# Attention of three branches in pairs of heads, and half of the modulation on VectorE

## The reference, cut to what matters

```python
mod = silu(c) @ w_mod[l] + b_mod[l]            # 6 x 1024: sh1, sc1, ga1, sh2, sc2, ga2; the same with c_ctx
h = rms_norm(x, norm1_g[l]) * (1 + sc1) + sh1
(..., gq, gk, gv, wq, wk, wv, nq, nk, nv, gate) = split_projection(h @ w_in)
out_a = mlstm(...)                             # branch A
out_b = softmax(q @ k.T * d**-0.5) @ v         # B: 8 heads of 64, 2 key heads, rms norm and rotary on q and k
out_c = ...                                    # C: the same in a window, with a sink logit in the softmax
out_d = ...                                    # D: 8 heads with their own keys, neighbourhood bias
y = sum_b sigmoid(gate_b) * (out_b @ w_branch[b]);  x = x + ga1 * (y @ w_out)
h2 = rms_norm(x, norm2_g[l]) * (1 + sc2) + sh2
x = x + ga2 * moe_ffn(h2)                      # 32 experts, top 2
```

## Time and profile before

| | us |
|---|---|
| median of 3 runs | 3130.76 (3129.21 to 3133.28) |
| profiled execution | 3133.22 |
| its span | 3131.6 |
| TensorE busy (share of span) | 2776.3 (89%) |
| VectorE busy | 894.6 (29%) |
| ScalarE busy | 420.0 (13%) |
| granted TensorE clock, mean | 0.94 |
| DMA | 623.62 MB, 199 GB/s |

### The profile page before, as it was taken

How to read it: one execution, slowest core, us unless ns; L and a number is a source line. 1 busy time by engine, 2 the same in 40 slices (tenths; PEclk the granted TensorE clock), 3 DMA queues, 4 the chain that set the end, 5 groups by cost and what they waited for, 6 DMA issues and landing times.

```text
span 3131.6 us, 43741 instructions
## 1 busy us (share of the span) xinstructions
PE 2776.3 (89%) x18152; PEld 1686.2 (54%) x18153; DVE 894.6 (29%) x2317; ACT 420.0 (13%) x960; POOL 148.9 (5%) x246
## 2 busy tenths in 40 slices
PE   4999899999999959999999889999999858777882
...
GB/s 270 54 54 54 68 32 59 41 54 54 74 47 236 96 134 376 381 380 376 379 384 382 269 93 54 81 94 51 108 115 163 219 203 396 393 402 394 403 400 142
DMA packets 148709, 623.62 MB, mean 199 GB/s; under 512 B 9329, under 2 KB 13697, under 8 KB 131713
## 3 DMA queue, kind: packets, MB, share of 16 engines
...
HBM read 596.94 MB, written 25.28 MB: 199 GB/s over the span
## 4 chain that ended last, share of the span: by engine, by line
PE 74%; DMA 16%; DVE 6%; issue 3%; ACT 1%; POOL 1%; SPq 0%; DVEq 0%; ACTq 0%; POOLq 0%
DMA ring<-in_e_up_dram 12%; PE bank L1378 11%; PE bank L1167 11%; PE bank L1077 10%; PE bank L1386 7%; PE bank L1067 6%; PE bank L1178 5%; PE bank L1095 5%; PE bank L1224 4%; PE bank L1254 4%; PE bank L1371 3%; PE bank L1236 2%; PE bank L1297 2%; DMA ring<-in_e_down_dram 1%; PE bank L1361 1%
## 5 line engine op out<-in xcount | busy, mean ns | idle before, releaser
L1378 PEld LDWEIGHTS bank<-scr,ring 128*64 128x64 f32 x8192 | 341.8, 138 | 25.9 <-issue 25.8
L1378 PE MATMUL bank<-scr,ring 128*64 128x96 f32 x8192 | 348.0, 247 | 1.2 <-DVE scr L2021 1.2
L1371 PE MATMUL bank<-ring,scr 128*64 128x256 f32 x2048 | 266.0, 419 | 89.4 <-DMA ring<-in_e_up_dram 70.3
L1167 PE MATMUL bank<-HT,ring 128*128 128x512 f32 (+1 forms) x1024 | 342.7, 490 | 0.0
L1077 PE MATMUL bank<-ring,HT 128*128 128x512 f32 (+1 forms) x800 | 303.6, 536 | 1.2 <-ACT ring L795 1.2
L1371 PEld LDWEIGHTS bank<-ring,scr 128*64 128x64 f32 x2048 | 156.8, 150 | 203.2 <-DMA ring<-in_e_up_dram 77.1
L1167 PEld LDWEIGHTS bank<-HT,ring 128*128 128x128 f32 x1024 | 191.3, 191 | 122.5 <-issue 110.1
L1386 PE MATMUL bank<-ring,scr 128*96 128x512 f32 x512 | 225.1, 592 | 0.8 <-issue 0.8
L1077 PEld LDWEIGHTS bank<-ring,HT 128*128 128x128 f32 x800 | 152.2, 194 | 134.3 <-issue 128.3
L1095 PE MATMUL bank<-ring,scr 128*128 128x512 f32 x384 | 175.8, 615 | 50.4 <-DMA ring<-in_w_mod_dram 34.8
L1067 PE MATMUL bank<-HT,ring 128*128 128x512 f32 (+1 forms) x512 | 199.1, 549 | 5.1 <-ACT scr L795 3.6
...
## 6 DMA issues: line engine op xcount, KB each, us to landing
ring<-in_e_up_dram SPq DMA_DIRECT2D x64, 2048.0 KB, 11.5
ring<-in_e_down_dram SPq DMA_DIRECT2D x64, 2048.0 KB, 11.6
ring<-in_e_gate_dram SPq DMA_DIRECT2D x64, 2048.0 KB, 9.2
ring<-in_w_in_dram SPq DMA_DIRECT2D x34, 2048.0 KB, 7.8
ring<-in_w_mod_dram SPq DMA_DIRECT2D x24, 2048.0 KB, 8.1
ring<-in_w_branch_dram SPq DMA_DIRECT2D x8, 2048.0 KB, 7.7
...
ring<-in_w_out_dram SPq DMA_DIRECT2D x4, 2048.0 KB, 7.9
```

Of the source, the lines that this page charges most:

```text
L1167: m = pe.matmul(bank[:, 0:NQ], w[:, k, (ft % 4) * P:(ft % 4) * P + P], HT[:, k, 0:NQ], start=k == 0, stop=k == KT_D - 1)
L1371: m = pe.matmul(ps[bank][hf * HALF:hf * HALF + cap, 0:256], XTv[:, k, :], w[:, k, hf * 256:hf * 256 + 256], start=k == 0, stop=k == KT_D - 1)
L1378: m = pe.matmul(ps[bank][rows_, f * cap:f * cap + cap], w[:, k, f * P + hf * HALF:f * P + hf * HALF + HALF], XTv[:, k, :], start=k == 0, s ...
```

## The change

- Stages D, B and C take heads in pairs. In D a pair is heads 2j and 2j+1, in B and C heads j and j+4, so that the two lie in the lower and the upper 64 partitions of the operands. A stage has 16 pair items in layer 0 and 8 in layer 1, and one step more than items.
- Scores: one matmul per head, each in its half of the array's rows, into two banks of one tile (`score_banks`). There is one pair of score banks, one buffer of P (`PB`) and one of turned P (`PTP`).
- P is scaled by the reciprocal before it is turned (`normalise`). ScalarE alone copies the turned blocks, both heads at once. The values are the stationary operand, 64 columns, each head in its half of the array's columns; the result is already transposed and VectorE copies it into `OT`. The `ot` transposes of D, B and C and their copies are gone. `OT` of D and C lies where `O` of stage A lay.
- Step i on TensorE: `turn(i-1)`, `scores(i)`, half of the due groups, `values(i-1)`, the other half.
- The eight `mod_b` groups are gone from stage C. VectorE multiplies rows of `w_mod` by `csil` and adds them up in `ACC`, 16 instructions of 512 columns per block in layer 0 (two vectors, 8 row groups each) and 8 in layer 1 (one vector, in two parts), four blocks in stage B and four in C. TensorE sums `ACC` over partitions with a matrix of ones. VectorE adds a row of `b_mod`, GpSimd stores the row to memory, and after all eight loads them back, spread over partitions.
- The third slot of the ring holds the two halves (1 MB each) of these blocks in stages B and C; the other weight blocks have two slots there. SP's order is sorted by the step in which a slot comes free. The value weights of B and C come in two transfers of 64 partitions. `out` 0 and 1 go to fixed slots.

```diff
-HOLD = {"A": 2, "D": 0, "B": 0, "C": 0}
-HEADS = {"A": MH, "B": 8, "C": 8, "D": 8}
+HOLD = {"A": 2}
+PAIRS = 4
...
+def sum_blocks(l, b):
+
+    if b not in "BC":
+        return []
+    todo = [(l, n) for n in range(4, 12)]
+    half = len(todo) // 2
+    return todo[:half] if b == "B" else todo[half:]
...
+def sum_span(l, b, j):
+
+    steps, n = stage_steps(l, b) - 1, len(sum_blocks(l, b))
+    return j * steps // n, (j + 1) * steps // n
...
+def sum_list(l, b, j):
+
+    m, n = sum_blocks(l, b)[j]
+    return [(k, part) for k in range(KT_D if m < L - 1 else KT_D // 2) for part in range(2)]
...
-        return value + gate + [("mod_b", n) for n in range(8)]
+        return value + gate
...
+def n_items(l, b):
+
+    return (MH if b == "A" else PAIRS) * q_tiles(l)
...
+    return n_items(l, b) + (2 + HOLD[b] if b == "A" else 1)
...
+        OT_B = br(6144, 2048).rearrange("p (j n) -> p j n", j=4)
+        OT = {"A": OT_A, "D": OT_B, "B": OT_A, "C": OT_B}
...
+        ACC = br(WK + 2048, 1024).rearrange("p (s n) -> p s n", s=2)
+        ROW = br(WK + 3072, 512)
...
+        SP_ = ctx.enter_context(nc.psum_tensor("score_banks", [P, 2, 512], F32))
+        PT_ = ctx.enter_context(nc.psum_tensor("turned_banks", [P, 2, 512], F32))
...
+                if slot is None:
+                    slot = sum(1 for k in BLOCK if k[0] == l) % (2 if key[1] in LATE else N_SLOT)
...
+            LATE = ("wq", "wk", "valD", "gateB", "valB", "gateC", "valC", "out")
...
+                slot = (1 - BLOCK[l, "valC"][0], N_SLOT - 1)[n]
...
+                def load_row(b, j):
+
+                    m, n = sum_blocks(l, b)[j]
+                    pool.dma_start(ROW, ins["b_mod"][m, n * 512:n * 512 + 512].partition_broadcast(P)).then_inc(row_loaded, 16)
+
+                def store_row(b, j):
+
+                    m, n = sum_blocks(l, b)[j]
+                    at = sum_index(l, b, j)
+                    pool.wait_ge(row_ready, at + 1)
+                    for s_ in range(2):
+                        pool.dma_start(mod_dram[m][s_:s_ + 1, n * 512:n * 512 + 512],
+                                       ROW[s_ * HALF:s_ * HALF + 1, :]).then_inc(row_stored, 16)
+                    pool.wait_ge(row_stored, 32 * (at + 1))
+
+                pool.wait_ge(o_ready, 4 * l + 2)
+                for b in "BC":
+                    for j in range(len(sum_blocks(l, b))):
+                        load_row(b, j)
+                        store_row(b, j)
+                for s_ in range(2 if l < L - 1 else 1):
+                    rows_ = slice(s_ * HALF, s_ * HALF + HALF)
+                    pool.dma_start(MODB[rows_, :], mod_dram[l][s_, 2 * D:5 * D].partition_broadcast(HALF)).then_inc(mod_loaded, 16)
+                    pool.dma_start(GA2[rows_, :], mod_dram[l][s_, 5 * D:6 * D].partition_broadcast(HALF)).then_inc(mod_loaded, 16)
...
+                    def turned_copy(i):
+
+                        c = c0 + i
+                        w = 512 if todo[i][1] < 2 else 256
+                        act.wait_ge(pair_turned, c + 1)
+                        if c:
+                            act.wait_ge(pair_out, c)
+                        act.activation(PTP[:, :, 0:w], PT_[:, :, 0:w], ACT.Copy).then_inc(pair_pt, 1)
+
+                    def exponentials(i):
+
+                        c = c0 + i
+                        lo = 0 if todo[i][1] < 2 else 256
+                        at = 2 * (c % 2)
+                        act.wait_ge(pair_peak, c + 1)
+                        if b == "C":
+                            act.activation(esink[:, at:at + 2], esink[:, at:at + 2], ACT.Exp)
+                        for hf in range(2):
+                            last = act.activation(PB[:, hf, 0:512 - lo], SP_[:, hf, lo:512], ACT.Exp, bias=nms[:, at + hf:at + hf + 1],
+                                                  scale=0.125, accum_out=rsum[:, at + hf:at + hf + 1])
+                        last.then_inc(pair_exp, 1)
...
+                def modulation_sum(b, j):
+                    pe.wait_ge(acc_ready, sum_index(l, b, j) + 1)
+                    both = l < L - 1
+                    def mms(bank):
+                        for s in range(2):
+                            at = s * HALF if both else 0
+                            m = pe.matmul(bank[at:at + HALF, :], ones[:, 0:HALF], ACC[:, s, :],
+                                          start=both or s == 0, stop=both or s == 1)
+                        return m
...
+                        lo = 0 if q < 2 else 256
+                        if c:
+                            pe.wait_ge(pair_exp, c)
+                        for hf in range(2):
+                            s = hf * HD
+                            k_ = KT_[s:s + HD, j, lo:512] if b == "D" else KT1[s:s + HD, lo:512]
+                            m = pe.matmul(SP_[:, hf, lo:512], QT_[s:s + HD, j, q * P:q * P + P], k_, start=True, stop=True)
+                        m.then_inc(pair_scored, 1)
+
+                    def turn(i):
+                        c = c0 + i
+                        pe.wait_ge(pair_p, c + 1)
+                        if c:
+                            pe.wait_ge(pair_pt, c)
+                        for hf in range(2):
+                            for k in range(4 if todo[i][1] < 2 else 2):
+                                m = pe.transpose(PT_[:, hf, k * P:k * P + P], PB[:, hf, k * P:k * P + P], ident)
+                        m.then_inc(pair_turned, 1)
+
+                    def values(i):
+                        j, q = todo[i]
+                        c = c0 + i
+                        pe.wait_ge(pair_pt, c + 1)
+                        if c >= 2:
+                            pe.wait_ge(pair_done, c - 1)
+                        tiles = range(4) if q < 2 else (2, 3)
+                        for n_, s in enumerate(tiles):
+                            for hf in range(2):
+                                at = j * P + hf * HD if b == "D" else P + hf * HD
+                                v = (V_ if b == "D" else KV)[:, s, at:at + HD]
+                                m = pe.matmul(ps[2 + c % 2][hf * HALF:hf * HALF + HALF, 0:P], v, PTP[:, hf, n_ * P:n_ * P + P],
+                                              start=n_ == 0, stop=n_ == len(tiles) - 1)
+                        m.then_inc(pair_out, 1)
+
+                    for i in range(n + 1):
+                        if i:
+                            turn(i - 1)
+                        if i < n:
+                            scores(i)
+                        if i == n and b in "DB":
+                            operands_transposed("B" if b == "D" else "C")
+                        for j in sums_at(l, b, i):
+                            modulation_sum(b, j)
+                        groups = due(l, b, i)
+                        half = (len(groups) + 1) // 2
+                        fill(b, groups[:half])
+                        if i:
+                            values(i - 1)
+                        fill(b, groups[half:])
...
+                def accumulate(b, j, ops):
+
+                    at = sum_index(l, b, j)
+                    both = l < L - 1
+                    for k, part in ops:
+                        if k == 0 and part == 0 and at:
+                            g = G[prev_sum(at)]
+                            dve.wait_ge(dense_full, g + 1)
+                        if sum_ops[0] >= 2:
+                            dve.wait_ge(acc_step, sum_ops[0] - 1)
+                        acc = ACC[:, part, :]
+                        c = csil[:, part if both else 0, (k if both else 2 * k + part):(k if both else 2 * k + part) + 1]
+                        row = k if both else 2 * k + part
+                        hf = row // 4
+                        dve.wait_ge(half_full[hf], HALF_BLOCK[l, b, j, hf])
+                        x = half_view(hf)[:, row % 4, :]
+                        if k == 0:
+                            m = dve.tensor_scalar(acc, x, c, None, ALU.mult)
+                        else:
+                            m = dve.scalar_tensor_tensor(out=acc, in0=x, scalar=c, in1=acc, op0=ALU.mult, op1=ALU.add)
+                        m.then_inc(acc_step, 1)
...
+                def sum_rows(b, i):
+
+                    for j in sums_at(l, b, i):
+                        at = sum_index(l, b, j)
+                        both = l < L - 1
+                        pn = P if both else HALF
+                        g = G[l, "sum" + b, j]
+                        bank = dense_wait(dve, g)
+                        dve.wait_ge(row_loaded, 16 * (at + 1))
+                        free_step(g, dve.tensor_tensor(ROW[0:pn, :], ROW[0:pn, :], bank[0:pn, :], ALU.add))
+                        dve.sem_inc(row_ready, 1)
...
+                        step(dve.tensor_reduce(nm[:, cols], SP_[:, :, lo:512], AX.X, ALU.max, negate=True))
...
+                    def normalise(i):
+
+                        j, q = todo[i]
+                        c = c0 + i
+                        w = 512 if q < 2 else 256
```

(44 more changed lines are left out.)

343 lines of the change are left out of this document (168 added, 175 removed).

## The result

The changed kernel took 2982.7 us (median of 4, 2980.8 to 2985.6) against 3132.0 us (3129.2 to 3137.7) for the kernel before on the same chip: a ratio of 0.952, 95% interval 0.951 to 0.954. The profiled execution took 2985.6 us, its span is 2984.0 (before 3131.6).

What follows compares the result with a forecast made beforehand. TensorE bounds the six attention stages: 739 us of work plus waits make 850, with clock (26) and value switches (7) 883 for 1001. With smaller moves the total is -121: 3010 us, range 2965 to 3055.

Steps and rivals of the forecast that it cites:

- wider overlap: Rival: score row halves run wholly side by side (-26 us), VectorE's multiply-adds take 0.69 (-12); 2972 us, chance 0.15.
- forecast case: The main prediction, with scores overlapping only partly and multiply-adds at 0.75 us; 3010 us, chance 0.58.
- Stage lengths: Six attention stages: 179, 187, 167 us in layer 0, 108, 114, 95 in layer 1; 850 in sum at full clock.
- value switches: Second change of array shape per step for value matmuls: 14 us if each costs what scores show; 7 taken.
- The waits of 111 us: TensorE's idle time in the six stages, mainly waiting for VectorE and the softmax chain; +31 and +7 in layer 0 C.
- The clock: TensorE's granted clock averages 0.97 over the six stages, as before; 26 us.
- Scores: Row halves of a pair's 512-column scores overlap in three slots of four: 1.29 + 0.2 us.
- VectorE in the value steps of C: VectorE's queue sets layer 0's value steps: 10.9 us, or 9.0 with 256 columns, against TensorE's 6.1.
- Stage B of both layers: Layer 0: single value blocks (+11) and turn of the operands (+6), 187 us; layer 1: +11, 114 us.
- sign of being wrong in kind: Stage B above 196 us, last wait before outputs for modulation rows or weights, or six-stage granted clock under 0.9.
- Slower: Rival: value and prepare steps end in gaps, next blocks run at half clock, mean 0.80; 3198 us, chance 0.06.
- chain and clock: Rival: softmax chain gaps lower TensorE's clock to 0.90 over the six stages, eating half the gain; 3078 us, chance 0.11.

Runs made afterwards that it cites:

- e4: Changed kernel with both heads of a pair scored from the first 64 partitions, in the same half of the array's rows (computes other scores); 3031.8 us.
- e2: Changed kernel with VectorE making only the first and last row group of each modulation block's running sum (leaves work out); 2944.0 us.
- e3: Changed kernel with half of each step's running-sum instructions moved between the peaks and the scaling of the same pair on VectorE; 2961.0 us.
- e7: Changed kernel with the ones matmuls that finish a modulation block moved behind the first half of the step's fill work; 2970.1 us.
- e8: Changed kernel with all running sums of stage C's four blocks moved to its gate half, none beside the values; 3004.9 us.
- e9: Changed kernel with stage C reordered: two value groups and one gate group in turn, then the other gates; 2981.7 us.

## Why the prediction was right, point by point

The sign, the order of the stages and the range (2965 to 3055) were right; the forecast of 3010 was 27 us too high, and the rival "wider overlap" (2972) lay nearer. What sets that rival apart from the forecast case is what came: row halves wholly side by side, and multiply-adds at 0.70 us. I had given it 0.15.

- **Stage lengths.** 845.5 us against 850: C of layer 0 was 11 us shorter than forecast, D of layer 1 9 us longer, the others within 4. This looks better than it is. The 850 were at full clock, with 26 for the low clock and 7 for the value switches still to come on top; the 845.5 hold both. Forecast with both, the stages were to take 883 us, and they took 38 less. Outside them I had taken 3 us off (5 for the transposes behind C, less 2), while the rest of the span came out 8 us longer than before (2138.5 for 2130.6, the span less the 1001). 38 less 11 is the 27 us of the whole error.
- **The waits of 111 us: the term that was mis-sized.** TensorE's busy time was forecast, with everything, at 739 + 26 + 7 = 772 us and was 772.7. Its idle time was forecast at 111 and was 72.8. So the 38 us are waits that didn't come. Of them 15 lie in C of layer 0, where the eight value steps took 67 us and not 80; 7 each in B of layer 0 and C of layer 1, 6 in D of layer 0 and 4 in B of layer 1.
- **The clock.** The mean granted clock of the six stages was 0.970, as forecast (0.971 before), and it cost TensorE 21 us, for 26 forecast. I had divided the waits by it too, which is wrong in kind but makes only 3 us (111 / 0.97 - 111). A slower TensorE also takes part of its extra time out of the waits: in e4 18 of the 69 us that it was busy longer. By that share, an estimate, some 5 of the 21 us were hidden so. It isn't what shrank the waits: stage B of layer 0 ran at 1.00 and had 7 us less of them than forecast, and D of layer 1, where the low clock cost 7 us, was as idle as forecast (12.8 for 12) and 9 us longer.
- **Scores.** 1.29 + 0.2 was too careful: 1.06, from 0.86 of streaming and 0.20 beyond it. It is the rival's price, worth 26 us by my own count. That the work was still 751 us and not less than my 746 (739 and the 7 for the value switches) has a plain reason: the dense blocks with the transposes of the operands came to 537 us at full clock, where I had 510 (124 + 124 + 83 + 69 + 69 + 41). The gates, projections and value blocks of stage D of layer 0 took 127 us before the change and 128 after it, for my 124. The 26 too many and the 27 too few cancel, and that was luck.
- **Values.** 54 ns forecast; 16 take 1.03 us, so 54 ns each and 0.17 beyond that: 72 x 0.17 = 12 us, between the 7 I took and the 14 at which I had priced the rule of the Trainium skill (TensorEngine Tiling, Key Properties) that a change of mode drains TensorE. The trace shows a small step at each change; that it is the change of shape that costs it, no run separates.
- **VectorE in the value steps of C.** 10.9 and 9.0 us forecast, 10.1 and 7.2 measured. The mechanism was right (scaling late, VectorE 76% busy there, no such wait in the gate half); the sizes were not: a multiply-add costs 0.70 from start to start, not 0.75, and in the pairs with 256 keys the wait for the exponentials is shorter. Four sums were then 2.8, and e2 and e3 show that they and their place, and not ScalarE's chain alone, set the length. TensorE was busy for 85% of stage C, where I had given 75 to 80% as the sign.
- **Stage B of both layers.** 187 and 114 forecast, 183.5 and 115.4 measured, but for a reason of which I named only a part: I wrote of single value blocks and the turn of the operands, and gave no price to TensorE's wait for the finished sum (6.9 us of the 9.8 idle in layer 0, 26 us in all). Whoever looks at the queues sees it ahead of time: VectorE does the last sums of a block at the end of its step, TensorE wants them early in the next.
- **The other moves.** The stretch behind stage C of layer 1 is 3 us longer, for 2 forecast. 2.5 of them lie in the expert loop, which took 585.1 us for 582.6 before and 581 to 588 in the experiments: scatter. The load of the output weights is the last wait ahead of the outputs there:

```profile
PE bank L1482 <- DMA ring<-in_w_out_dram: 1.9, 1, 1.9
```

  I had named such a wait as a sign of being wrong in kind. It came, but it is 1.9 us, where before TensorE waited 1.0 us for VectorE at this place, so the sign was set too sharp. The blocks themselves took 15.0 us to landing in the median instead of 7.9:

```profile
ring<-in_w_out_dram SPq DMA_DIRECT2D x4, 2048.0 KB, 15.0
```

  Two now start together, beside the modulation rows that come back from memory; what that costs is what e7 showed. The loads of the half blocks of `w_mod` (5.2 us for 1 MB) hid, as forecast.
- **"Slower" and "chain and clock".** Neither came, but their mechanism exists. In e8 and e9 a gate took 8.9 to 9.2 us for 7.06 behind light stretches, and one misplaced group of sums cost 22 us. In the changed kernel itself eight transposes took 1.97 us for 1.09 behind the wait in the first step of C:

```profile
770.39 1.97 PE L1364 MATMUL turned_banks<-consts,scr 128*128 128x128 f32 x8 [5.34 <-DVE scr L2076]
```

  No run went as far as the 0.80 of that rival; the lowest stage was at 0.89.
